# Three of four channel chunks of a 31-tap depthwise convolution as 32x32 diagonal products on TensorE, in place of 47 products of 128x128 and VectorE taps

## The reference

```python
def causal_dwconv(u, w):                # w: 31 taps x 512 channels, one filter for each channel
    k = w.shape[0]
    return lax.conv_general_dilated(
        u, w[:, None, :], window_strides=(1,), padding=[(k - 1, 0)],
        dimension_numbers=("NWC", "WIO", "NWC"), feature_group_count=u.shape[-1])

def pool_conv_mixer(h, w_in, pool_w, pool_scale, dw_w, dw_b, ln_g, ln_b, w_out):
    z = h @ w_in
    u, glu_a, glu_b = jnp.split(z, [POOL_W, POOL_W + CONV_W], axis=-1)       # 512, 512, 512
    ...                                  # windows of 2, 4, 8, 16 tokens over u, then pool_w: ya
    gl = glu_a * jax.nn.sigmoid(glu_b)
    cv = causal_dwconv(gl, dw_w) + dw_b
    yb = jax.nn.silu(layernorm(cv, ln_g, ln_b))
    return jnp.concatenate([ya, yb], axis=-1) @ w_out
```

## Time and profile before

| | |
|---|---|
| three runs | 2385.61, 2385.51, 2381.87 us; median 2385.51 us |
| the profiled execution's own time | 2383.48 us |
| its span in the trace | 2381.6 us |
| mean granted TensorE clock | 0.997 |

### The profile page before, as it was taken

One profiled execution on the slowest core, in us unless ns is written; L12 is line 12 of the kernel. 1 busy time (PEld: TensorE's weight loads), 2 busy tenths in 40 slices (PEclk: granted clock), 3 DMA queues, 4 the chain that ended last, 5 costly groups with the idle time before them and its releaser, 6 DMA issues.

```text
span 2381.6 us, 29066 instructions
## 1 busy us (share of the span) xinstructions
PE 2348.1 (99%) x10762; PEld 1864.9 (78%) x10762; DVE 1218.8 (51%) x2026; ACT 939.8 (39%) x1418; POOL 997.2 (42%) x744
## 2 busy tenths in 40 slices
PE   8999999999999999999999999999999999999999
PEld 6777778878888888757878888887667877888887
DVE  4454545244433346794457555556774243655544
ACT  3355444334222227424444222225875443322222
POOL 4323335223544545635525545444113233545443
PEclk9999999999999999999999999999999999999999
DMA  5212322422323223223213232222013521332231
GB/s 174 78 64 94 91 89 89 159 71 93 102 92 106 88 97 99 89 70 98 79 58 106 89 106 88 97 97 77 29 36 100 166 71 62 107 99 95 88 106 71
DMA packets 170087, 218.69 MB, mean 92 GB/s; under 512 B 6585, under 2 KB 144107, under 8 KB 169975
## 3 DMA queue, kind: packets, MB, share of 16 engines
q1 hardware_dynamic: 168278, 214.59, 27.6%
q10 hardware_dynamic: 1696, 2.61, 0.3%
HBM read 215.05 MB, written 2.12 MB: 91 GB/s over the span
## 4 chain that ended last, share of the span: by engine, by line
PE 89%; DVE 4%; ACT 3%; issue 1%; POOL 1%; DMA 1%; SPq 0%; DVEq 0%; ACTq 0%
PE ps_l L964 79%; PE ps_l L1383 2%; PE ps_l L1113 1%; PE ps_s L1366 1%; ACT w_hi L1628 1%; POOL w_lo L810 1%; PE ps_s L1470 1%; DVE small L3025 1%; DVE arena L3017 1%; PE ps_s L1485 1%; PE ps_s L1263 1%; PE ps_s L1307 0%; PE ps_s L964 0%; DVE small L3027 0%; PE ps_l L1248 0%
## 5 line engine op out<-in xcount | busy, mean ns | idle before, releaser
L810 POOL TENSOR_TENSOR w_lo<-w_raw,w_hi 128x512 fp32r<-128x512 f32 (+1 forms) x740 | 997.0, 1378 | 1363.2 <-ACT w_hi L1628 1340.5
L964 PE MATMUL ps_l<-a_hi,w_hi 128*128 128x512 f32 x1936 | 762.9, 394 | 3.9 <-POOL w_lo L810 2.9
L964 PE MATMUL ps_l<-a_lo,w_hi 128*128 128x512 f32 x1952 | 758.4, 389 | 0.0
L964 PE MATMUL ps_l<-a_hi,w_lo 128*128 128x512 f32 x1936 | 754.0, 389 | 0.0
L1628 ACT ACTIVATE w_hi<-w_raw 128x2048 fp32r<-128x2048 f32 (+2 forms) x196 | 370.6, 1891 | 598.5 <-PE ps_l L964 575.7
L964 PEld LDWEIGHTS ps_l<-a_hi,w_hi 128*128 128x128 f32 x1936 | 362.7, 187 | 89.9 <-issue 10.9
L964 PEld LDWEIGHTS ps_l<-a_lo,w_hi 128*128 128x128 f32 x1952 | 365.9, 187 | 78.4 <-issue 3.1
L964 PEld LDWEIGHTS ps_l<-a_hi,w_lo 128*128 128x128 f32 x1936 | 362.7, 187 | 76.9
L964 PE MATMUL ps_l<-b_hi,w_hi 128*128 128x512 f32 (+1 forms) x892 | 330.3, 370 | 6.7 <-issue 2.3
L964 PE MATMUL ps_l<-b_lo,w_hi 128*128 128x512 f32 (+1 forms) x892 | 327.3, 367 | 0.0
L964 PE MATMUL ps_l<-b_hi,w_lo 128*128 128x512 f32 (+1 forms) x892 | 327.2, 367 | 0.0
(11 more groups left out here) (308 smaller groups left out, 2420.5 us busy)
## 6 DMA issues: line engine op xcount, KB each, us to landing
w_raw<-in_ffn_w_up_dram SPq DMA_DIRECT2D x44, 1024.0 KB, 5.1
w_raw<-in_w_dram SPq DMA_DIRECT2D x32, 1024.0 KB, 5.2
w_raw<-in_ffn_w_down_dram SPq DMA_DIRECT2D x22, 1024.0 KB, 4.9
w_raw<-in_w_in_dram SPq DMA_DIRECT2D x20, 1024.0 KB, 5.4
w_raw<-in_xa_wkv_dram SPq DMA_DIRECT2D x16, 1024.0 KB, 5.5
w_raw<-in_w_kv_mem_dram SPq DMA_DIRECT2D x8, 1024.0 KB, 5.7
w_raw<-in_xa_wq_dram SPq DMA_DIRECT2D x8, 1024.0 KB, 5.1
w_raw<-in_xa_wo_dram SPq DMA_DIRECT2D x8, 1024.0 KB, 5.2
```

Of the source, the lines that this page charges most:

```text
L810: e.tensor_tensor(w_lo[:, b % 2, o], w_raw[:, b % 2, o], w_hi[:, b % 2, o].bitcast(F32), ALU.subtract).then_inc(w_lo_made[by], 1)
L964: ins = pe.matmul(o, *((v, w) if swap else (w, v)), start=first and n == 0, stop=last and n == 2)
```

## The change

Chunks 1, 3 and 2 go to PE whole, in this order, and chunk 0 stays with DVE. A 128x128 diagonal matrix has only four 32x32 blocks on its diagonal that are not zero. Each tap of a chunk becomes four products of 32 rows by 32 columns, one for each group r of 32 channels. Tap j writes into bank s = (j + 1) % 4 of the S ring, at the 32 partitions (r + s) % 4. So four taps that follow each other use all sixteen places of the 128x128 array, and each bank holds the sum of every fourth tap, its channel groups turned by s places.

What else moves:

- `conv_taps(0)` stands ahead of the first block of `pool_u`, `conv_taps(1)` between the two, `conv_taps(2)` behind them. Each claims four groups of the S ring.
- ACT no longer makes diagonals. `part_id` (four copies of 32x32) is made once; `conv_out(n)` copies the banks 1 to 3 to SBUF, four ACTIVATEs of 32x512 each, turning the groups back. It stands on ACT's queue ahead of the `hi` call for the block after next, and from the second on waits for `conv_sum`.
- DVE makes the diagonals of a chunk in one `tensor_tensor` of 31x32 columns, three in all, and `conv_add(n)` adds the four parts in three steps. It has 31 taps left, all of chunk 0, each of which waits for the tap before.

```diff
-    S.add("conv3", "v")
-    S.add("conv2", "v")
+    for q in PE_CHUNKS:                       # (1, 3, 2)
+        S.add(f"conv{q}", "vaaa")
...
-            stage("pool_u", xa, nb=2)
+            def conv_taps(n):
+                q = PE_CHUNKS[n]
+                g = S.base[f"conv{q}"]
+                pe.wait_ge(glu_r, q + 1)
+                pe.wait_ge(diag_r, n + 1)
+                for s in range(4):
+                    claim(pe, S, g + s)
+                for j in range(CONV_K):
+                    s = (j + 1) % 4
+                    for r in range(4):
+                        rows, out = slice(32 * r, 32 * r + 32), 32 * ((r + s) % 4)
+                        ins = pe.matmul(bank(S, g + s)[out:out + 32, :], diag(n)[rows, j, :], gl[rows, q, j:j + T],
+                                        start=j < 4, stop=j >= CONV_K - 4)
+                    if j >= CONV_K - 4:
+                        ins.then_inc(s_full, 1)
+            conv_taps(0)
+            feat(b, g, 8, 256, xa)
+            conv_taps(1)
+            feat(b + 1, g + 2, 8, 256, xa)
+            conv_taps(2)
             stage("xk1+", xm, nb=1, n=MEM)
...
-            diags()
-            just_hi("pool_u", 2)
+            conv_out(0)
+            hi(b + 2)
+            conv_out(1)
+            hi(b + 3)
+            conv_out(2)
             block_copies("xk1+", 1, 2, lambda j: kT[:, 6 + j, :], cols=MEM)
-            shared_diags()
...
+            def conv_out(n):
+                if n:
+                    act.wait_ge(conv_sum, n)
+                for s in (1, 2, 3):
+                    g = S.base[f"conv{PE_CHUNKS[n]}"] + s
+                    wait_group(act, S, g)
+                    for r in range(4):
+                        c = (r + s) % 4
+                        ins = act.activation(conv_part(s)[32 * r:32 * r + 32, :], bank(S, g)[32 * c:32 * c + 32, :], ACT.Copy)
+                    ins.then_inc(s_free["a"], 1)
```

More of the change, by code:

```diff
@@ L426 @@
 PI32 = 3.1415925
[L427 to L447, removed]
+DVE_CHUNK = 0
+PE_CHUNKS = (1, 3, 2)
 U = {"diff": 0, "fox": 16, "xa0": 48, "xa1": 64, "mla0": 80, "mla1": 112, "xa2": 144}
@@ L552, in build @@
         ck8 = sb("ck8", [P, TT * 8])[:, :]
+        part_id = sb("part_id", [P, 32])[:, :]
         GKV = (COL["g_mem_kv"], COL["norm_mem_g_2"], COL["norm_mem_g_2"] + 8)
@@ L1462, in _ @@
             stage("glu", xa, ready=h_ready(4), behind={0: both_sums})
-            stage("pool_u", xa, nb=2)
-            stage("xk1+", xm, nb=1, n=MEM)
[L1465 to L1473, removed]
+            def conv_taps(n):
[13 more added lines that the diff above has]
+                        ins.then_inc(s_full, 1)
+            b, g = plan.block_base["pool_u"], L.base["pool_u"]
+            conv_taps(0)
[3 more added lines that the diff above has]
+            conv_taps(2)
+            stage("xk1+", xm, nb=1, n=MEM)
             g = L.base["pool_w"]
@@ L1480, in _ @@
                     .then_inc(l_full, 1)
[L1481 to L1487, removed]
             b, g = plan.block_base["pc_out_a"], L.base["pc_out_a"]
@@ L1491, in _ @@
             claim(pe, S, g)
-            pe.wait_ge(tap, TAPS)
-            wait_read(pe, S, S.base["conv2"])
+            pe.wait_ge(tap, CONV_K)
+            pe.wait_ge(conv_sum, len(PE_CHUNKS))
             for q in range(4):
@@ L2060, in _ @@
             hi(plan.block_base["glu"] + 2)
[L2062 to L2074, removed]
+            def conv_out(n):
[8 more added lines that the diff above has]
+                    ins.then_inc(s_free["a"], 1)
+            for r in range(0, P, 32):
+                act.activation(part_id[r:r + 32, :], ident[r:r + 32, r:r + 32], ACT.Copy).then_inc(part_id_r, 1)
             g, b = L.base["glu"], plan.block_base["glu"]
@@ L2771, in _ @@
             glu_in(1, 0)
+            dve.wait_ge(part_id_r, 4)
+            for n, q in enumerate(PE_CHUNKS):
+                w = COL["conv_dw_w_2"] + q
+                dve.tensor_tensor(diag(n), part_id.unsqueeze(1).broadcast_to((P, CONV_K, 32)),
+                                  cols[:, w:w + 4 * CONV_K - 3:4].unsqueeze(2).broadcast_to((P, CONV_K, 32)), ALU.mult)\
+                    .then_inc(diag_r, 1)
             tap_n = [0]
             def taps(upto):
-                for n in range(tap_n[0], min(upto, TAPS)):
-                    j, q, before = TAP_ORDER[n]
+                q = DVE_CHUNK
+                for j in range(tap_n[0], upto):
                     w = col("conv_dw_w_2", 4 * j + q)
@@ L2781, in taps @@
                     else:
-                        dve.wait_ge(tap, before + 1)
+                        dve.wait_ge(tap, j)
                         ins = dve.scalar_tensor_tensor(out=cvt[:, q, :], in0=gl[:, q, j:j + T], scalar=w,
@@ L2803, in _ @@
                 step(dve.tensor_tensor(dst[:, 0:m, st:UW], src[:, 0:m, st:UW], src[:, 0:m, st - d:UW - d], ALU.add))
-                taps(28 + 4 * (n + 1))
+                taps(12 + n + 1)
                 sync()
@@ L2812, in _ @@
                                          in1=up_[:, q, 16:UW], op0=ALU.mult, op1=ALU.subtract).then_inc(pool_r, 1)
-            taps(60)
+            taps(20)
+            conv_add(2)
             for q in range(4):
@@ L2820, in _ @@
                     .then_inc(l_free["v"], 1)
[L2821 to L2830, removed]
+            taps(CONV_K)
             def pool_out(ns):
```

35 lines of the change are left out of this document (26 added, 9 removed).

## The result

| | before | after |
|---|---|---|
| median, us | 2383.69 (2380.47 to 2385.61, 4 runs) | 2399.60 (2396.25 to 2402.37, 4 runs) |
| span of the profiled execution, us | 2381.6 | 2397.2 |

The ratio is 1.0069, with a 95% interval of 1.0057 to 1.0082: **slower by 16 us**, where 10 us less had been forecast. The forecast had the wrong sign, and the time lies 1.6 us above the upper end of its range.

What follows compares the result with a forecast made beforehand. PE was taken to bound the kernel, with DVE close behind. From 2383.48 us, `pc_out_a` 11.7 us earlier less 1.7 us of clock loss gave 2373.5 us; the range was 2367 to 2398, the forecast's own 2367 to 2378.

Steps and rivals of the forecast that it cites:

- What costs nothing: ACT's copies end in time, the last eleven taps end as `ln_mean` is reached, and everything after is as before.
- sum off elsewhere: Catch-all: an order of DVE and POOL other than drawn; chance 0.08, of it 0.02 slower.
- Sixteen at once: In PE's conv chunks, all sixteen 32x32 places of the array work side by side at full speed.
- Rivals 1 to 4: Chunk length: fewer streams, 10 to 13 us (0.22); issue, 15.4 (0.12); one row tile per bank, 26.6 (0.10); program order, 53 (0.06).
- c = 7.2 us: PE's time for one conv chunk: eight rounds of 0.85 us and 0.4 us to start and drain.
- The waits of 1.2 us for POOL: PE's waits for POOL's remainders in the second block of `pool_u` go, since the extra chunks give POOL room.
- The second block ends at 1031.0: PE's second `pool_u` block ends at 994.8 + 2c + 21.8 = 1031.0, against 1017.8 before.
- 24.3 us on DVE from there to the first `A_lo` read: DVE's steps from the end of `pool_u`'s second block through the first `A_lo` take 24.3 us.
- `pc_out_a` 11.7 us earlier: PE's `pc_out_a` starts at 1055.3 instead of 1066.96.
- PE stands still for 6.5 us, and loses 1.7 for the clock: PE idles 6.5 us ahead of `pc_out_a`; the lowered clock behind it costs 1.7 us, bounds 0 and 3.4.
- ACT's twelve copies, 7.2 us, never late: Twelve copies of 0.60 us per chunk end before PE leaves the next `pool_u` block, so `hi` is not late.
- Sum of - 10.0: Whole kernel: - 11.7 + 1.7 = - 10.0 us on the profiled execution's 2383.48, giving 2373.5 us.

Runs made afterwards that it cites:

- e1: Kernel before plus an unused tensor of 128 bytes per partition where the change puts `part_id`: 2403.65 us, ratio 1.0087.
- the moved run: Changed kernel with `part_id` allocated last, so every other tensor keeps its address from the kernel before: 2377.14 us, ratio 0.9974.
- e8: The moved run's kernel with every small product of the conv chunks over 256 columns instead of 512: 2373.62 us, one run.
- e7: The moved run's kernel with DVE's taps reordered to fill its waits for ACT's copies, no instruction added: 2371.79 us, ratio 0.9958.
- e5: Kernel before plus an unused 128 bytes per partition ahead of `w_raw`, shifting weights and A2 but not x, A, B: 2407.09 us, ratio 1.0103.
- e6: Kernel before plus an unused tensor of 64 bytes per partition at the place of `part_id`: 2395.21 us, ratio 1.0058.
- e9: The moved run's kernel with a chunk's taps ordered bank by bank, so successive products ask for the same four places: 2406.94 us, one run.
- e3: Kernel before plus an unused tensor of 256 bytes per partition at the place of `part_id`: 2382.14 us, ratio 0.9998.
- e4: Kernel before plus an unused 128 bytes per partition ahead of the first tensor, shifting everything together: 2381.78 us, ratio 0.9995.
- e10: e7's kernel with DVE's taps moved further forward and `part_id` back in its place, padded to 256 bytes per partition: 2368.55 us, ratio 0.9938.

## Why the prediction was wrong

**The step that failed** is in "What costs nothing": "From there everything is as before." It was false ahead of the stage and behind it. The diff's line that allocates `part_id` was read as a name for the diagonals' input and given no price, because it issues no instruction. It shifted A2 against the weights by 128 bytes, and that costs 20.7 us by e1. The rivals all looked for the loss among the new products. But PE is busy 99% of the span, so some 7 ns more on each product that reads A2 count in full, and no rival asked what the diff does to those. The "sum off elsewhere" had a chance of 0.02 for slower, and its cause was not this.

**The terms of the stage**, from the moved run, whose trace stands 1.6 us behind that of before when it reaches the stage (the clock was at half over six products near 13 us):

- *Sixteen at once*: right. Rivals 1 to 4 fall: not two streams, not issue (e8), not one row tile to a bank, not the program's order. Four row tiles of one tap write one bank side by side.
- *c = 7.2 us*: measured 8.64 (996.59 + 0.23 to 1005.46 in the moved run). "Eight rounds of 0.85 us" left out the reload, 0.22 a round. Two chunks lie on the path: 2.9 us.
- *The waits of 1.2 us for POOL* are gone, as forecast.
- *The second block ends at 1031.0*: 1034.5 by the clock of before, 2.9 from the chunks and some 0.6 in the blocks and between them.
- *24.3 us on DVE from there to the first `A_lo` read*: 25.3. Its steps came in another mix than forecast (the first sum 2.35 where 3.4 stood, the taps beside POOL 1.75), and the total held.
- *`pc_out_a` 11.7 us earlier*: 7.1 us. 2.9 + 0.6 + 1.0 make the 4.5 that are missing (11.7 - 7.1, but for rounding).
- *PE stands still for 6.5 us, and loses 1.7 for the clock*: 6.9 us, and 2.2 us.
- *ACT's twelve copies, 7.2 us, never late*: 7.24 us each time. PE was not late for them, but DVE was: its sums waited 5.6 us in all for them, a wait that the plan of "when a chunk is full" passed over. It cost nothing by itself, since DVE would have waited for `pool_u` behind it, but it is where e7 found room.
- *Sum of - 10.0*: the stage gives - 7.1 + 2.2 = - 4.9 by the traces, - 5.8 by the medians. So without the address the gain is some half of the forecast, and the moved run's 2377.1 lies just inside the forecast's own range (2367 to 2378).

What stays open: why the price lies in the relation of operand and weights modulo 256 bytes. And the slow start: near 13 us six products take 0.63 us each in some traces (after, the moved run, e5, e6, e9) and 0.39 in others (before, e1, e3, e4, e7, e10). 0.63 us is also their length at the granted clock of 0.50 behind PE's gap in the moved run. This is worth some 1.5 us and was not looked into.

## What to carry to other kernels

Treat every allocation in the middle of the memory as a possible change to all that lies behind it: pad new tensors so that streamed operands and the weights they meet keep their distance modulo 256 bytes, and compare the mean duration of the commonest product before and after, also in stages that weren't touched. An unused pad in the old kernel separates the address from the edit in one run. Compare the changed stage in the traces too, from one mark to another: stretches at half clock elsewhere differ between the traces here and move the whole (by 2.8 us in e10). When small tiles are packed, put the products of different places next to each other, and count the reload for each round when all places are busy; and when an engine becomes late, look for its idle time earlier in the stage before adding anything.

## What was not expected of the hardware

- float32r products with 512 columns, weights and moving data at different places modulo 256 bytes: one every 233.3 ns in place of 226.7 at 128 bytes apart, 3%; nothing at 0 or 256; less than at 128, and not for every pair of tensors, at 64.
- Sixteen 32x32 places take sixteen float32 products at once, the starts within 0.1 us (16 under way in 996.90:997.10), and reach 12.3 times one place's speed.
- A place's reload is hidden with four places busy and is not with sixteen: 21.8 us against 8.6 for the same 248 pieces. By the streams alone it would be 26.6 against 6.8; a stretch of some 5 us with eight places busy and the exposed reload make the difference.
